# Conditioning pieces fetched in the order 0, 2, 1, 3, and a token product cut in two over its depth

## The reference, cut to what matters

```python
cond = jax.nn.silu(c)                                  # (1, 1024)
ada = (cond @ w_ada + b_ada)[:, None, :]               # (1, 1, 6144)
sh1, sc1, g1, sh2, sc2, g2 = jnp.split(ada, 6, axis=-1)
h = rms_norm(x, norm1_g) * (1.0 + sc1) + sh1           # (512, 1024)
p = h @ w_in
q, ckv, qi, ki, wi, a_pool, gate_a, gate_b = jnp.split(p, SPLIT_OFFSETS, axis=-1)
```

## Time and profile before

| what | value |
|---|---|
| median of 3 runs | 987.86 us (985.82 to 988.47) |
| the profiled execution, its own time | 986.01 us |
| its span in the profile | 984.3 us |
| TensorE busy | 944.8 us, 96% of the span |
| TensorE weight load busy | 510.3 us, 52% |
| VectorE busy | 403.8 us, 41% |
| ScalarE busy | 227.2 us, 23% |
| GpSimd busy | 198.2 us, 20% |
| mean DMA rate | 289 GB/s, 283.96 MB moved |

### The profile page before, as it was taken

One profiled execution on the slowest core, in us unless ns is written; L12 is line 12 of the kernel. 1 busy time (PEld: TensorE's weight loads), 2 busy tenths in 40 slices (PEclk: granted clock), 3 DMA queues, 4 the chain that ended last, 5 costly groups with the idle time before them and its releaser, 6 DMA issues.

```text
span 984.3 us, 16925 instructions
## 1 busy us (share of the span) xinstructions
PE 944.8 (96%) x7152; PEld 510.3 (52%) x7152; DVE 403.8 (41%) x832; ACT 227.2 (23%) x488; POOL 198.2 (20%) x240
## 2 busy tenths in 40 slices
PE   3999989999999999999999999999999999999995
PEld 2676656667788757544444444443444444344442
DVE  0275968744633565324423223242322323233255
ACT  6334344444322314111101111010111101111112
POOL 2222942103300001212121211112121111211002
PEclk9999989999999999999999999999999999999998
DMA  9927624720432658999999999999999999999915
GB/s 340 346 88 256 210 71 149 256 86 17 134 124 86 256 214 300 358 347 380 379 356 382 398 376 396 383 391 388 385 396 373 398 384 380 377 377 394 383 45 184
DMA packets 71443, 283.96 MB, mean 289 GB/s; under 512 B 7488, under 2 KB 8796, under 8 KB 54984
## 3 DMA queue, kind: packets, MB, share of 16 engines
q1 hardware_dynamic: 61720, 257.93, 68.0%
q0 software_dynamic: 9648, 24.94, 9.6%
HBM read 272.62 MB, written 18.56 MB: 296 GB/s over the span
## 4 chain that ended last, share of the span: by engine, by line
PE 87%; DMA 5%; DVE 4%; issue 2%; SPq 1%; ACT 1%; POOL 0%; POOLq 0%; DVEq 0%; ACTq 0%
PE ps L1766 22%; PE ps L1501 19%; PE ps L1798 11%; PE ps L1777 11%; PE ps L1788 5%; PE ps L1723 3%; PE ps L1712 2%; DMA ring<-in_w_ada_dram 2%; PE ps L1753 2%; PE ps L1553 2%; PE ps L1625 2%; PE ps L1865 2%; PE ps L1532 1%; PE ps L1761 1%; DMA apad<-h_rows,iug 1%
## 5 line engine op out<-in xcount | busy, mean ns | idle before, releaser
L1330 DVE TENSOR_SCALAR mix<-ps 128x384 f32<-128x384 f32 x32 | 17.9, 558 | 344.0 <-ACT attn L993 344.0
L1501 PE MATMUL ps<-h_hi,wb_hl 128*128 128x512 f32 x384 | 126.0, 402 | 0.0
L705 POOL DMA_INDIRECT moe_rows<-mix,ius x31 | 50.9, 1642 | 243.8 <-DVE mix L1379 141.3
L993 ACT ACTIVATE attn<-ps 128x384 f32<-128x384 f32 x32 | 15.7, 491 | 306.9 <-PE ps L1777 306.9
L1501 PEld LDWEIGHTS ps<-h_hi,wb_hl 128*128 128x128 f32 x384 | 72.4, 189 | 20.4 <-issue 5.0
L1501 PE MATMUL ps<-h_lo,wb_hl 128*128 128x512 f32 x192 | 75.0, 391 | 0.0
L1371 DVE SCALAR_TENSOR_TENSOR mix<-ps,WC,attn 32x256 f32<-32x256 f32 x128 | 61.6, 481 | 7.2 <-PE ps L1788 4.9
L1379 DVE SCALAR_TENSOR_TENSOR mix<-ps,WC,attn 64x512 f32<-64x512 f32 x64 | 47.8, 747 | 34.4 <-PE ps L1798 33.4
L1766 PE MATMUL ps<-ring,mix 128*64 128x512 f32 x272 | 59.9, 592 | 0.0
L1766 PE MATMUL ps<-ring,uvp 128*64 128x512 f32 x256 | 56.9, 592 | 0.0
L624 POOL TENSOR_TENSOR wb_hl<-ring,wb_hl 128x1024 fp32r<-128x1024 f32 x16 | 38.6, 2419 | 84.2 <-ACT wb_hl L832 67.5
(11 more groups left out here) (308 smaller groups left out, 1527.5 us busy)
## 6 DMA issues: line engine op xcount, KB each, us to landing
ring<-in_w_gu_dram SPq DMA_DIRECT2D x66, 1024.0 KB, 16.2
ring<-in_w_down_dram SPq DMA_DIRECT2D x30, 1024.0 KB, 11.1
ring<-in_w_ada_dram SPq DMA_DIRECT2D x12, 2048.0 KB, 11.7
area_b<-in_w_gu_dram SPq DMA_DIRECT2D x16, 1024.0 KB, 14.7
hT<-in_w_gu_dram SPq DMA_DIRECT2D x16, 1024.0 KB, 16.7
X<-in_w_gu_dram SPq DMA_DIRECT2D x16, 1024.0 KB, 16.8
area_a<-in_w_gu_dram SPq DMA_DIRECT2D x14, 1024.0 KB, 16.5
ring<-in_w_in_dram SPq DMA_DIRECT2D x6, 2048.0 KB, 8.0
```

Source lines behind the costliest of these rows:

```text
L705: pool.indirect_dma_start(out=y_dram, in_=Y[0:slots, b, :], in_offset=None, out_offset=bass.IndirectOffsetOnAxis(ap=which, axis=0), bounds ...
L1501: last = mm(out_, a, b, start=(n == 0 and start_), stop=(n == len(pairs) - 1))
```

## The change

The order of the pieces becomes `a0, a2, tok, a1, a3, q`, with slots 0, 2, 0, 1, 3, 1, so that `tok` waits for `a0` to be used, `q` for `a1`, and `a1` and `a3` for nothing. `kvgb` stays behind `a3`, and POOL's first transfers wait for `a3` in place of `tok`. On TensorE `ada_part(0)` stands before the transposes of `xn`, `ada_part(2)` behind them, and the hum of 20 is gone. The column sums, the modulation on VectorE, the rounding to `h_hi` on ScalarE and `h_lo` are each cut into a half for features 0 to 511 and a half for the others. All four token banks are opened together. The first half of the depth of each token chunk is multiplied first, with `ada_part(1)`, `ada_part(3)` and their columns in between, and the second half of all four chunks after that. The sums and their number of instructions are the same except for three more small instructions on VectorE and 20 hum matmuls fewer.

```diff
-        PIECES = ([("a", j, ada_piece(j)) for j in range(4)]
-                  + [("tok", 0, in_piece(COL_TOK, TOKW)), ("q", 0, in_piece(COL_Q, AW))]
+        PIECES = ([("a", 0, ada_piece(0)), ("a", 2, ada_piece(2)), ("tok", 0, in_piece(COL_TOK, TOKW))]
+                  + [("a", 1, ada_piece(1)), ("a", 3, ada_piece(3)), ("q", 0, in_piece(COL_Q, AW))]
...
-        slot_of = [0, 1, 2, 3, 0, 1] + [2, 0, 1] + [2, 0, 2] + [1, 2, 1] + [2, 2] + [0] + [2, 1] + [0] + [2, 1]
-        before = [None if n < FR else max(m for m in range(n) if slot_of[m] == slot_of[n])
-                  for n in range(len(PIECES))]
+        slot_of = [0, 2, 0, 1, 3, 1] + [2, 0, 1] + [2, 0, 2] + [1, 2, 1] + [2, 2] + [0] + [2, 1] + [0] + [2, 1]
+        before = [max((m for m in range(n) if slot_of[m] == slot_of[n]), default=None) for n in range(len(PIECES))]
...
         JOBS = ([("sv", 0, "D")]
-                + [("xT", i, "A") for i in range(8)]
-                + [("ada", j, "A") for j in range(4)] + [("adac", 0, "D")]
+                + [("ada", 0, "A")] + [("xT", i, "A") for i in range(8)]
+                + [("ada", 2, "A"), ("ada", 1, "A"), ("ada", 3, "A"), ("adac", 0, "D")]
...
             for n, (kind, i, src) in enumerate(PIECES):
-                if n >= FR:
+                if before[n] is not None:
                     used(before[n])
                 sp.dma_start(piece(kind, i), src).then_inc(piece_in[slot_of[n]], 16)
-                if n == 3:
+                if n == 4:
                     sp.dma_start(kvgb[:, :], spread(kv_norm_g[0], LAT)).then_inc(kvg_in, 16)
...
-            front_came(pool, "tok")
+            front_came(pool, "a", 3)
...
+            ada_copy(0)
             for i in range(8):
                 ch, half = i // 2, i % 2
                 nc.scalar.activation(hT[:, 4 * half:4 * half + 4, ch * P:(ch + 1) * P],
                                      job("xT", i).rearrange("p (k t) -> p k t", k=4), ACT.Copy).then_inc(by_act, 1)
...
-            for j in range(4):
-                ada_copy(j)
+            ada_copy(2)
             act.wait_ge(xn_ok, C)
-            act.wait_ge(hT_ok, KD)
-            for k in range(KD):
-                last = nc.scalar.activation(h_hi[:, k, :], hT[:, k, :], ACT.Copy)
-            last.then_inc(h_hi_ok, 1)
+
+            def h_high(half):
+                act.wait_ge(hT_ok, KD // 2 * (half + 1))
+                for k in range(KD // 2 * half, KD // 2 * (half + 1)):
+                    last = nc.scalar.activation(h_hi[:, k, :], hT[:, k, :], ACT.Copy)
+                last.then_inc(h_hi_ok, 1)
+
+            h_high(0)
+            ada_copy(1)
+            ada_copy(3)
+            h_high(1)
...
+            dve.wait_ge(half_cols_done, 1)
+            modulation(0, half_A1_ok)
+            dve.wait_ge(half_A1_ok, 1)
+            dve.wait_ge(by_act, emptied[number["xT", 7]])
+            h_rows(0)
+            h_low(0)
+            job("adac")
+            modulation(1, by_vec)
             dve.wait_ge(by_vec, emptied[number["adac", 0]])
...
+            h_rows(1)
+            h_low(1).then_inc(h_lo_ok, 1)
...
-            for j in range(4):
-                ada_part(j)
-            b_ = start("adac")
-            for j in range(4):
+            ada_part(2)
+            cols = start("adac")
+
+            def ada_cols(j):
+
                 emptied_by("ada", j)
                 for q in range(4):
...
+            ada_cols(0)
+            ada_cols(2).then_inc(half_cols_done, 1)
             w = have("tok")
-            for ch in range(C):
-                b_ = start("tok", ch)
-                if ch == 0:
-                    hum(b_, 8)
-                for k in range(KD):
+            toks = [start("tok", ch) for ch in range(C)]
+
+            def tok_part(ch, ks):
+
+                for k in ks:
                     pe.wait_ge(hT_ok, k + 1)
...
+            hum(toks[0], 8)
+            tok_part(0, range(0, 4))
+            tok_part(1, range(0, 4))
+            ada_part(1)
+            tok_part(2, range(0, 4))
+            ada_part(3)
+            ada_cols(1)
+            tok_part(3, range(0, 2))
+            ada_cols(3).then_inc(job_done, 1)
+            tok_part(3, range(2, 4))
+            for ch in range(C):
+                tok_part(ch, range(4, KD)).then_inc(job_done, 1)
```

More of the change, by code:

```diff
@@ L233, in trunk @@
                      for i in range(2)])
-        FR = 4
-        slot_of = [0, 1, 2, 3, 0, 1] + [2, 0, 1] + [2, 0, 2] + [1, 2, 1] + [2, 2] + [0] + [2, 1] + [0] + [2, 1]
-        before = [None if n < FR else max(m for m in range(n) if slot_of[m] == slot_of[n])
-                  for n in range(len(PIECES))]
+        slot_of = [0, 2, 0, 1, 3, 1] + [2, 0, 1] + [2, 0, 2] + [1, 2, 1] + [2, 2] + [0] + [2, 1] + [0] + [2, 1]
+        before = [max((m for m in range(n) if slot_of[m] == slot_of[n]), default=None) for n in range(len(PIECES))]
         NFP = len(PIECES)
@@ L312, in trunk @@
         c_ok = sem("c_ok")
+        half_cols_done, half_A1_ok = sem("half_cols_done"), sem("half_A1_ok")
         job_done = sem("job_done")
@@ L809, in _, with ada_copy @@
                                      scale=rstd[:, ch:ch + 1]).then_inc(xn_ok, 1)
+            def ada_copy(j):
+                nc.scalar.activation(acc[j], job("ada", j), ACT.Copy).then_inc(by_act, 1)
+            ada_copy(0)
             for i in range(8):
@@ L813, in _ @@
                                      job("xT", i).rearrange("p (k t) -> p k t", k=4), ACT.Copy).then_inc(by_act, 1)
-            def ada_copy(j):
-                nc.scalar.activation(acc[j], job("ada", j), ACT.Copy).then_inc(by_act, 1)
-            for j in range(4):
-                ada_copy(j)
+            ada_copy(2)
             act.wait_ge(xn_ok, C)
-            act.wait_ge(hT_ok, KD)
-            for k in range(KD):
-                last = nc.scalar.activation(h_hi[:, k, :], hT[:, k, :], ACT.Copy)
-            last.then_inc(h_hi_ok, 1)
+            def h_high(half):
[7 more added lines that the diff above has]
+            h_high(1)
             def block_high(n):
@@ L1080, in _ @@
             v.tensor_copy(svT[:, :], job("sv")[:, 0:28]).then_inc(by_vec, 1)
[L1082 to L1086, removed]
-            dve.wait_ge(by_vec, emptied[number["adac", 0]])
-            dve.wait_ge(by_act, emptied[number["xT", 7]])
@@ L1089, in _, with modulation @@
-            for k in range(KD):
[L1090 to L1096, removed]
+            def modulation(half, done):
+                b_ = bank("adac")
+                at = slice(4 * half, 4 * half + 4)
+                v.tensor_tensor(sh1c[:, at], b_[:, 4 * half:4 * half + 4], svT[:, at], ALU.add)
+                link(v.tensor_tensor(A1[:, at], b_[:, 8 + 4 * half:12 + 4 * half], svT[:, 8 + 4 * half:12 + 4 * half], ALU.add))
+                v.scalar_tensor_tensor(out=A1[:, at], in0=A1[:, at], scalar=1.0, in1=svT[:, 16 + 4 * half:20 + 4 * half],
+                                       op0=ALU.add, op1=ALU.mult).then_inc(done, 1)
@@ new lines, in h_rows, with h_low @@
+            def h_rows(half):
+                for k in range(4 * half, 4 * half + 4):
+                    v.tensor_scalar(hT[:, k, :], hT[:, k, :], A1[:, k:k + 1], sh1c[:, k:k + 1], ALU.mult,
+                                    ALU.add).then_inc(hT_ok, 1)
+            def h_low(half):
+                dve.wait_ge(h_hi_ok, half + 1)
+                for k in range(4 * half, 4 * half + 4):
+                    last = v.tensor_tensor(h_lo[:, k, :], hT[:, k, :], h_hi[:, k, :], ALU.subtract)
+                return last
@@ L1098, in _ @@
+            dve.wait_ge(by_vec, emptied[number["sv", 0]])
+            dve.wait_ge(half_cols_done, 1)
[6 more added lines that the diff above has]
+            modulation(1, by_vec)
+            dve.wait_ge(by_vec, emptied[number["adac", 0]])
+            h_rows(1)
+            h_low(1).then_inc(h_lo_ok, 1)
             dve.wait_ge(kvg_in, 16)
@@ L1513, in _, with ada_part @@
             nc.tensor.transpose(start("sv")[:, 0:28], sv[:, :], ident[0:28, 0:28]).then_inc(job_done, 1)
+            def ada_part(j):
+                b_ = start("ada", j)
+                w = have("a", j)
+                pe.wait_ge(c_ok, 1)
+                for k in range(KD):
+                    at = 32 * (k % 4)
+                    last = mm(b_[at:at + 32, :], cnd[:, 2, k:k + 1].broadcast_to([P, 32]), w[:, k, :], start=(k < 4),
+                              stop=(k >= 4), tile_position=(0, at))
+                last.then_inc(job_done, 1)
+            ada_part(0)
             for i in range(8):
@@ L1521, in _ @@
                 last.then_inc(job_done, 1)
[L1523 to L1534, removed]
@@ L1536, in _ @@
-            for j in range(4):
-                ada_part(j)
-            b_ = start("adac")
-            for j in range(4):
+            ada_part(2)
+            cols = start("adac")
+            def ada_cols(j):
                 emptied_by("ada", j)
                 for q in range(4):
```

(19 more changed lines are left out.)

## The result

| | before | after |
|---|---|---|
| median, 6 runs each | 988.02 us (985.1 to 988.55) | 982.15 us (980.95 to 983.24) |
| the profiled execution's span | 984.3 us | 979.7 us |

The ratio is 0.9945, with a 95% interval of 0.9925 to 0.9966. That is 5.4 us less, or 5.9 by the medians. The prediction was 981.8 us, with a range of 979.0 to 985.8. A second measurement of the same kernel beside the experiments gave 0.9955 (0.9937 to 0.9973).

The account below looks back on a forecast made before the run. TensorE's line was taken to bound the kernel, with a gap waiting for `a3`. Dividing the token product gains 5.6 us, its faster rate 0.4, together 6.0; from the 987.9 median, 981.9, predicted as 981.8 us, range 979.0 to 985.8.

Parts of the forecast that it names:

- What bounds, and the gap: Whole kernel: one line of TensorE work; its gap at the start is the wait for `a3`, 24.2 us from landing to `uk`.
- The start of the first half: Front part: first token matmul at 27.8 us, after `ada_part(0)`, transposes, `ada_part(2)`, columns and modulation.
- ScalarE decides: Before the first half: ScalarE's copies, ending at 24.5 and 25.1 us, set the pace, not TensorE's transposes.
- Transfers: Front part: `tok` lands by about 23.7 us, `a3` at 35.9 (34.2 to 38), `a1` by 29 to 30.
- There is no hole: Transfer stream near 20 us: `tok`, issued by 18.4, flows at 20.0 while `a2` is under way until 20.15.
- The token product: Token stage: second half starts at 42.2 us, ends at 50.9; 5.6 us gained, 6.0 with a faster matmul rate of 0.52.
- No slow stretch: Token stage: no new low-clock stretch counted, since TensorE has no wait over about 1 us between 22 and 50.
- Rival 3: Token stage: clock stays at 1.2 GHz, costing 9.1 us, so 3.1 us slower at 991.0; chance 0.03.
- Worth nothing by itself: Front part: removing the hum of 20 gains nothing, since TensorE only waited there.
- What comes next: Behind the token product: everything moves 6 us forward, so the gain is kept to the end.
- Both tight places: After the token product: token banks emptied at 50.4 us, wanted at 51; `a4` in at 49.8, wanted at 51.5.
- Rival 2: Behind the front: a stretch with its own date or a clock fall gives back 4 to 6 us; chance 0.07.

Follow-up runs that it names:

- VectorE's copies: Changed kernel with the copies of `ada` 0 and `ada` 2 on VectorE instead of ScalarE; ratio 0.9952 to the kernel before.
- the free slot: Changed kernel with `a0` in slot 3 and `tok` in unused slot 0, so `tok` is issued at once; ratio 0.9952 to the kernel before.
- the early hum: Changed kernel plus a hum of 20 behind the first transpose, while TensorE waits for `a0`; ratio 0.9928, median 979.69 us.
- three edits and the early hum: Changed kernel with `tok` in free slot 0, `ada` 0 and 2 copied on VectorE, `ada_part(3)` behind two chunk-3 matmuls, plus early hum of 20; ratio 0.9916, median 978.60 us.

## Why the prediction was right

**What bounds, and the gap.** Right. The link from `a3` to `uk` is 50.30 - 36.27 = 14.0 us, where it was 24.2. A later `a3` moves `uk` one for one (2.5 us and 2.5 us).

**The start of the first half.** Predicted 27.8, measured 27.23. ScalarE's part was right (24.5 and 25.1 us forecast, 24.46 and 24.96 measured), and `ada_part(0)` ended at 18.3, the end of the bounds that I took. What I had too long were the columns, which TensorE had begun under ScalarE's copy. But "ScalarE decides" was only half true, as VectorE's copies showed.

**Transfers.** "There is no hole" was wrong. I took the landing of `a2` at 20.15 as the time until which the ring is busy. It landed at 20.1, but the rate was down to 127 GB/s from 19 us on: most of the data were in sooner, and those of `tok`, issued at 18.39, weren't flowing yet. The price was 0.6 us by the free slot. The Trainium skill, "DMA: Bandwidth & Descriptors", section "Anatomy of one DMA", puts a transfer's fixed cost at about 2.0 us, from which I had estimated a hole of 0.25 us. The trace agrees with it that there is one, but not with its size or its start: the hole begins a us ahead of the landing of `a2`. `a3` was forecast at 35.9 from the row of `tok`, and `ada_part(3)` began at 36.27, so the row gave nearly the right number, though the stream has a hole now that it did not have when the row was made. That is in part luck.

**The token product.** Half a product of 2.17 us, `ada_part` of 1.85, columns of 0.9: right. The second half was forecast to start at 42.2 and took up its full pace at 42.16, and 32 records took 8.15 us, 0.51 a matmul, where 0.542 stood in the first sum and 0.52 in the second. `uk` at 50.30 is the lower end of 50.3 to 51.

**No slow stretch.** Right in the trace, but the reason that I gave, that TensorE has no long wait, is not enough. In this kernel it was the hum of 8 that kept the clock, as the run without it shows. I costed it at nothing but cover. It is no safe means either: with the early hum the clock fell in spite of it. Rival 3 was nearer than 0.03 says, even if its full price of 9 us appeared nowhere: one such stretch cost 1.7 us on the spot.

**The hum of 20.** "Worth nothing by itself" holds for the time (1.0019, 0.9999 to 1.0039) and not for the trace. Without it the kernel before had `uk` 1.6 us sooner, and its `pool` piece took 0.8 us longer. The sum has neither.

**What comes next.** Both tight places held. The token banks were emptied at 50.3 and `ada_part(4)` (51.40) had its piece. Rival 2 came true for about 1 us: the `pool` piece is released by TensorE, but its duration changed, through a fetch of instructions of which the working knew nothing. A shorter slow stretch gave 0.8 us back later.

**The time.** A gain of 6.0 us was forecast. By the medians it was 5.9, by the ratio 5.4. The front part bears the forecast out on its own (6.2 us at `uk`). That the end agrees as well is partly luck, since the loss of 1.1 us and the return of 0.8 us were both outside the sum.

## What to carry to other kernels

A reduction that waits for a late operand can be cut over its depth so that the work that doesn't need the operand comes first, but it pays only if the transfers are put in the order of that work: here each half of the change alone cost 4 to 6 us, and both together won 5 to 6. A transfer that is issued just before the last one lands can leave a hole, because most of the last one's data may be in long before it has landed: here the rate was a third of the usual for the last us. Matmuls that nobody uses are to be judged by the clock in the stretch behind them, and by what their instructions move, not by the wait that they fill.

## What the runs showed of the hardware

A fetch of 16 KB of instructions that falls within a transfer of 2 MB delays its landing: it was 8.4 to 9.3 us from issue to reader in nine traces with a fetch inside, 7.7 to 7.8 us in four without. 40 matmul and weight-load instructions more or fewer on TensorE moved the fetch by 5 to 6 us relative to `uk`. An edit that seems free can so change the time of a transfer some 50 to 60 us later.

The clock can fall to 1.2 GHz although work goes on. In the run with three edits and the early hum TensorE had no wait between 27 and 40 us, but ahead of 39 us it did eight matmuls with one column of output each (sixteen records), and the clock then read 0.50 from 41 to 43 us. With sixteen such matmuls in one block it fell each time: in the kernel before (at 38.6 us), without its hum of 20 (36.2) and with the new order alone (39.3). With eight in one block it fell in the one place told here, and at the same place without the early hum it stayed at 1.00. So such matmuls stand ahead of these falls, but the runs don't show that they are the cause.
